# Matrices ahead, lag products, odd gates and the last norm of a two-layer mixer and expert trunk

## The reference, cut to what matters

```python
for i in range(2):
    hn = rms_norm(h, norm_mix[i])
    h = h + (chunked_rel_attention(hn, ...) if i == 0 else s5_mixer(hn, ...))
    hn = rms_norm(h, norm_ffn[i])
    h = h + hierarchical_moe(hn, ..., w_gate[i], w_up[i], w_down[i])
return rms_norm(h, norm_final)          # h * rsqrt(mean(h*h) + 1e-6) * g

# hierarchical_moe, after routing (best of 4 groups, best 2 of its 8 experts)
for e in range(32):
    hid = silu(t @ w_gate[e]) * (t @ w_up[e])      # 1024 x 256 each
    out = out + gates[:, e:e + 1] * (hid @ w_down[e])   # 256 x 1024

# s5_mixer: 64 groups of 16 channels, each with 64 complex states
abar = exp((lambda_re + 1j * lambda_im) * step)
bbar = (abar - 1) / lambda * b
x_t = abar * x_(t-1) + bbar @ u_t ; y = Re(c @ x) + d * u
```

## Time and profile before

| | us |
|---|---|
| median of 3 executions | 711.55 (710.52 to 712.64) |
| profiled execution | 711.8 |
| its span on the core | 710.1 |
| PE busy in the span | 629.6 (89%) |
| share of the chain that ended last: PE, DMA, SP | 72%, 19%, 3% |
| mean granted clock of PE, of full speed | 0.942 |

### The profile page before, as it was taken

How to read it: one execution, slowest core, us unless ns; L and a number is a source line. 1 busy time by engine, 2 the same in 40 slices (tenths; PEclk the granted TensorE clock), 3 DMA queues, 4 the chain that set the end, 5 groups by cost and what they waited for, 6 DMA issues and landing times.

```text
span 710.1 us, 13191 instructions
## 1 busy us (share of the span) xinstructions
PE 629.6 (89%) x5567; PEld 404.3 (57%) x5567; DVE 193.9 (27%) x499; ACT 136.7 (19%) x301; POOL 190.2 (27%) x226
## 2 busy tenths in 40 slices
PE   7999999999999988989598889999999798796583
PEld 5888888876556656456163654456564365353140
DVE  3234233254231023103022770235203023002003
ACT  3111313232021011011014511122220012010003
POOL 1001120250699997970961000030000000000001
PEclk9999999999998999899799999997999999898688
DMA  9997976665999999999999379964899999999992
GB/s 313 344 327 148 366 214 222 254 242 220 414 420 405 393 423 421 420 422 421 423 389 381 127 241 420 422 255 174 323 425 368 422 419 420 420 421 420 420 397 80
DMA packets 86707, 244.20 MB, mean 344 GB/s; under 512 B 28053, under 2 KB 56949, under 8 KB 62581
## 3 DMA queue, kind: packets, MB, share of 16 engines
q1 hardware_dynamic: 85188, 237.50, 86.7%
q0 software_dynamic: 1056, 5.24, 1.9%
q10 hardware_dynamic: 400, 0.57, 0.3%
HBM read 239.08 MB, written 4.22 MB: 343 GB/s over the span
## 4 chain that ended last, share of the span: by engine, by line
PE 72%; DMA 19%; SPq 3%; ACT 2%; DVE 1%; issue 1%; POOL 0%; DVEq 0%; POOLq 0%; ACTq 0%
DMA ring<-in_moe_w_down 11%; PE ps L2002 10%; DMA ring<-in_moe_w_up 9%; PE ps L1722 8%; PE ps L2289 8%; PE ps L2042 7%; PE ps L1856 7%; PE ps L2062 4%; PE ps L1725 4%; PE ps L1783 4%; PE ps L1702 3%; PE ps L1852 2%; SPq L478 2%; PE ps L1823 1%; PE ps L1918 1%
## 5 line engine op out<-in xcount | busy, mean ns | idle before, releaser
L2002 PE MATMUL ps<-ring,xg 128*32 128x256 f32 x1808 | 120.9, 402 | 26.3 <-DMA ring<-in_moe_w_up 14.5
L2002 PEld LDWEIGHTS ps<-ring,xg 128*32 128x32 f32 x1808 | 66.4, 116 | 74.3 <-issue 47.1
L2042 PE MATMUL ps<-ring,hidT 128*32 128x512 f32 x488 | 67.5, 671 | 15.8 <-DMA ring<-in_moe_w_down 10.6
L2062 PE MATMUL ps<-y_sb,pickT 128*128 128x512 f32 x128 | 59.5, 605 | 3.4 <-DVE y_sb L1475 1.7
L861 POOL TENSOR_TENSOR xh<-x,normw 128x1024 f32<-128x1024 f32 x1 | 2.4, 2352 | 214.2 <-DVE x L1437 214.2
L1722 PE MATMUL ps<-xnT,ring 128*128 128x256 f32 x256 | 57.7, 381 | 1.0 <-ACT xnT L904 1.0
L2289 PE MATMUL ps<-ring,yT 128*128 128x512 f32 x128 | 55.6, 594 | 0.9 <-ACT yT L1087 0.9
L1722 PEld LDWEIGHTS ps<-xnT,ring 128*128 128x128 f32 x256 | 47.8, 190 | 8.6 <-ACT xnT L904 1.2
L1442 DVE TENSOR_TENSOR hid<-sg,ps 128x256 f32<-128x256 f32 (+1 forms) x18 | 7.2, 399 | 156.2 <-ACT sg L1004 143.6
L2042 PEld LDWEIGHTS ps<-ring,hidT 128*32 128x32 f32 x488 | 17.4, 121 | 50.7 <-issue 43.3
L1856 PE MATMUL ps<-pick,xn 128*128 128x256 f32 x192 | 44.0, 382 | 0.0
(11 more groups left out here) (376 smaller groups left out, 878.1 us busy)
## 6 DMA issues: line engine op xcount, KB each, us to landing
ring<-in_moe_w_up SPq DMA_DIRECT2D x59, 1024.0 KB, 17.2
ring<-in_moe_w_gate SPq DMA_DIRECT2D x57, 1024.0 KB, 13.2
ring<-in_moe_w_down SPq DMA_DIRECT2D x53, 1024.0 KB, 16.2
ring<-in_attn_w_qkv SPq DMA_DIRECT2D x11, 1024.0 KB, 11.6
ring<-in_moe_w_down SPq DMA_DIRECT2D x16, 512.0 KB, 12.5
ring<-in_ssm_w_out SPq DMA_DIRECT2D x8, 1024.0 KB, 12.4
ring<-in_attn_w_o SPq DMA_DIRECT2D x4, 1024.0 KB, 10.9
chunk_inputs<-turned POOLq DMA_DIRECT2D x3, 1024.0 KB, 11.1
```

The costliest lines, as they stand in the source:

```text
L2002: ins = mm(ps[CAP * h:CAP * (h + 1), GUB, F * half:F * (half + 1)], p.xg[:, c, CAP * (ROUND * r + h):CAP * (ROUND * r + h + 1)], w, start= ...
L2042: ins = mm(ps[CAP * h:CAP * (h + 1), DNB + b, :], hidT[:, r, j, CAP * h:CAP * (h + 1)], w, start=(j == 0), stop=(j == FT - 1), tile_positi ...
L2062: ins = mm(ps[:, u, :], p.pickT[rows, r, tt * P:(tt + 1) * P], y_sb[rows, r, 512 * b:512 * (b + 1)], start=(r == 0), stop=(r == p.rounds - 1))
```

## The change

**Layer 0.** Three MiB more are on chip ahead of the first turns: a gate and an up of turn 0 (`fore_gate`, `fore_up`) and two half ups of turn 1 (`fore_up_next`). The ring slot they leave takes turn 1's matrices early.

**Layer 1.** Turn 0's second gate goes to `fore_gate`, and two half ups of turn 1 go to places that are free by then; one MiB net. From turn 3 on, odd turns' gates go outside the ring, into the places of turn 1's matrices, and gates are loaded two turns ahead (`turn + 2`).

**Lag products.** They are interleaved with the ups of the octets' first rounds: piece 0 in turn 2, piece 2 in turn 4, piece 3 in turn 6; piece 1 in the gather of the spill pass. Four of them stand ahead of each four wide products (eight ahead of each two in the spill pass). PE waits for the piece's table first. The table is turned right behind the ups. Turn 7 of layer 0 now starts with the sum, then gates, `keep_warm`, ups. POOL's work is put in another order.

**Final norm.** In layer 1's turn 7 PE first multiplies the identity with `x[:, tt, 512:]` into banks 1 and 3, and the last sums are added on top; ACT squares these columns out of PSUM, and DVE scales them out of PSUM. The norm's weights are multiplied by -0.5 by POOL ahead of time, which spares a step.

```diff
-WARM = {"start": 2, "choice": (5, 3), "ranks": 1, "regrouping": 1, "last lags": 4}
+WARM = {"start": 2, "choice": (5, 3), "ranks": 1, "regrouping": 1, "last up": 4}
...
+        fore_gate = at("fore_gate", [P, MAT], 6656)
+        fore_up = [(at("fore_up0", [P, MAT // 2], 4096), normw), (q4, normw)]
+        fore_up_next = (q4, at("fore_up_next", [P, MAT // 2], 10784))
...
+        def odd_gates(layer, turn):
+            return layer == 1 and turn >= 3 and turn % 2 == 1
+        odd_gate = [ahead_gu[1][:, 0:MAT], ahead_gu[1][:, MAT:], ahead_gu_next[:, 0:MAT], ahead_gu_next[:, MAT:]]
...
+                    elif not layer and s == RING - 1:
+                        gate_up(layer, first + ROUND + s, s, 0, slot_full[s])
+                    elif not (layer and s == 1):
...
+                def load_gate(at, e):
+                    turn, s = at
+                    if odd_gates(layer, turn):
+                        sp.dma_start(odd_gate[s], wg[:, bass.ds(E * layer + e, 1), :].rearrange("p o n -> p (o n)")).then_inc(odd_full, 16)
+                    else:
+                        gate_up(layer, e, s, 0, slot_full[s])
                 def places(turn, full):
                     kept = ahead_slots(full, layer, 1)
-                    if layer and full is slot_full and turn < 2:
-                        return [(2, s) for s in reversed(range(1, RING))] if turn == 0 else [(2, 0)]
+                    if layer and full is slot_full:
+                        if turn < 2:
+                            return [(2, 3), (2, 2)] if turn == 0 else [(2, 0)]
+                        return [(turn + 2, s) for s in range(RING)] if turn + 2 < 2 * NO else []
                     if turn == 0:
-                        return [(1, s) for s in range(kept, RING)] + [(2, s) for s in reversed(range(kept))]
+                        return [(1, s) for s in range(kept, RING) if not first_elsewhere(full, layer, s)]\
+                            + [(2, s) for s in reversed(range(kept))]
                     return [(turn + 1, s) for s in range(kept if turn == 1 else 0, RING)]
                 def load_behind(turn):
                     gates, ups, downs = (places(turn, full) for full in (slot_full, second_full, down_full))
-                    expert = {at: expert_at(*at) for at in dict.fromkeys(gates + ups)}
+                    behind_ups = [(3, s) for s in range(RING)] if layer and turn == 1 else []
+                    expert = {at: expert_at(*at) for at in dict.fromkeys(gates + ups + downs + behind_ups)}
                     held = turn == BLOCK_TURN
                     sp.wait_ge(S.first_done, k0 + turn + 1)
                     for at in gates[held:]:
-                        gate_up(layer, expert[at], at[1], 0, slot_full[at[1]])
+                        load_gate(at, expert[at])
                     sp.wait_ge(S.gu_done, k0 + turn + 1)
                     for at in ups[held:]:
-                        rows = slice(MAT // 2, MAT) if at == (1, 1 + layer) else slice(0, MAT)
+                        rows = slice(MAT // 2, MAT) if at == (1, 2 + layer) else slice(0, MAT)
                         gate_up(layer, expert[at], at[1], 1, second_full[at[1]], rows)
+                    for at in behind_ups:
+                        load_gate(at, expert[at])
...
+                if not layer:
+                    e = first + RING - 1
+                    sp.dma_start(fore_up[0][0][:], wu[:, e, 0:MAT // 2]).then_inc(fore_full, 16)
+                    sp.wait_ge(rows_ready, 2)
+                    sp.dma_start(fore_up[0][1][:], wu[:, e, MAT // 2:MAT]).then_inc(fore_full, 16)
+                    sp.wait_ge(ms_ready, 2)
+                    sp.dma_start(fore_up_next[0][:], wu[:, first + ROUND + 1, MAT // 2:MAT]).then_inc(ahead_full, 16)
                 if layer:
+                    sp.wait_ge(rows_ready, 5)
+                    sp.dma_start(fore_up[1][1][:], wu[:, E * layer + first + ROUND + 3, 0:MAT // 2]).then_inc(ahead_full, 16)
+                    sp.wait_ge(ms_ready, 4)
+                    sp.dma_start(fore_up[1][0][:], wu[:, E * layer + first + ROUND + 2, MAT // 2:MAT]).then_inc(ahead_full, 16)
...
+                if layer:
+                    gate_up(layer, expert_at(2, 1), 1, 0, slot_full[1])
...
+                pool.wait_ge(lags_evac, i + 1)
                 pool.wait_ge(tab_evac, 2 * (i + 1))
...
-            chunk_outputs((0, 1))
+            chunk_outputs((0,))
             store_inputs(0)
             chunk_inputs(1)
-            chunk_outputs((2,))
-            steps()
-            tables((1, 2, 4, 8))
+            chunk_outputs((1, 2))
             store_inputs(1)
             chunk_inputs(2)
-            tables((16,))
+            steps()
+            tables((1, 2))
             store_inputs(2)
             chunk_inputs(3)
+            tables((4, 8, 16))
...
+                    ins = nc.scalar.activation(xn[:, tt, 512:D], x[:, tt, 0:512], ACT.Square, accum_out=small[:, 7, tt:tt + 1])
+                ins.then_inc(rms_ready, 1)
+                act.wait_ge(main.comb_done, 4 * (2 * NO - 1) + 3)
+                nc.scalar.activation(xn[:, 0, 0:512], ps[:, 1, :], ACT.Square, accum_out=small[:, 0, 0:1])
+                act.wait_ge(main.comb_done, 4 * 2 * NO)
+                nc.scalar.activation(xn[:, 1, 0:512], ps[:, 3, :], ACT.Square, accum_out=small[:, 0, 1:2]).then_inc(rms_ready, 1)
...
+            def final_norm():
+                ss, ms, rt, r0, t1, rs, part = (small[:, j, :] for j in (0, 1, 2, 3, 5, 6, 7))
+                dve.wait_ge(rms_ready, 6)
+                lk(V.tensor_scalar(part, part, 1.0 / D, EPS, ALU.mult, ALU.add))
+                dve.wait_ge(rms_ready, 7)
+                V.scalar_tensor_tensor(out=ms, in0=ss, scalar=1.0 / D, in1=part, op0=ALU.mult, op1=ALU.add).then_inc(ms_ready, 1)
+                dve.wait_ge(rms_ready, 8)
+                lk(V.reciprocal(r0, rt))
+                for tt in range(TT):
+                    one = slice(tt, tt + 1)
+                    ins = V.scalar_tensor_tensor(out=t1[:, one], in0=ms[:, one], scalar=r0[:, one], in1=r0[:, one],
+                                                 op0=ALU.mult, op1=ALU.mult)
+                lk(ins)
+                V.scalar_tensor_tensor(out=rs, in0=t1, scalar=-3.0, in1=r0, op0=ALU.add, op1=ALU.mult).then_inc(rs_ready, 1)
+                dve.wait_ge(rs_ready, 3)
+                dve.wait_ge(rows_ready, 6)
+                for tt in range(TT):
+                    V.scalar_tensor_tensor(out=xn[:, tt, 512:D], in0=ps[:, 2 * tt + 1, :], scalar=rs[:, tt:tt + 1], in1=normw[:, 512:D],
                                            op0=ALU.mult, op1=ALU.mult).then_inc(xn_ready, 1)
...
+                        if beside:
+                            lag_products(beside, (2 * c, 2 * c + 1))
...
-            def lag_products(i, banks):
-
-                pe.wait_ge(tab_ready, i + 1)
-                for st in range(JP):
+            def lag_products(p, sts):
+                i = p.piece(0)
+                for st in sts:
                     for r in range(2):
-                        for par_g, bank in enumerate(banks):
+                        for par_g, at_lags in enumerate(lag_places(p)):
                             rows = slice(NS * par_g, NS * (par_g + 1))
-                            ins = mm(ps[:, bank, GC * st:GC * (st + 1)], wbt[rows, st, r].rearrange("p m c -> p (m c)"),
+                            ins = mm(at_lags[:, GC * st:GC * (st + 1)], wbt[rows, st, r].rearrange("p m c -> p (m c)"),
                                      wC[rows, 0, r, JP * i + st, :], start=(r == 0), stop=(r == 1), tile_position=(NS * par_g, 0))
-                return ins
+                    if st == JP - 1:
+                        ins.then_inc(lags_done, 1)
...
-                def gate_up(r, half, done):
+                def gate_up(r, half, done, beside=None):
                     for c in range(KT):
+                        if beside:
+                            lag_products(beside, (c,))
...
+                    if p.layer and p.closes(r):
+                        pe.wait_ge(before_p.S.x_added, 4 * before_p.n + 4)
+                        for tt in range(TT):
+                            mm(ps[:, 2 * tt + 1, :], ident, x[:, tt, 512:D], start=True, stop=False)
...
+                    sums_first = p.layer == 0 and p.closes(r)
+                    if sums_first:
                         pe.wait_ge(S.yh_done, p.k + r)
                         pe.wait_ge(S.yl_done, p.k + r)
-                        keep_warm(GUB, WARM["last lags"])
-                        lag_products(3, (DNB, DNB + 1)).then_inc(tab_turned, 1)
                         pe.wait_ge(before_p.S.x_added, 4 * before_p.n + 4)
-                        turn_chunk_inputs(0)
+                        combine(r - 1)
...
-                        if p.layer == 0 and p.closes(r):
-                            pe.wait_ge(tab_evac, 8)
-                        combine(r - 1)
+                        if sums_first:
```

(16 more changed lines are left out.)

204 lines of the change are left out of this document (110 added, 94 removed).

## The result

| | before | after |
|---|---|---|
| median | 711.12 us | 729.38 us |
| span of the profiled execution | 710.1 us | 726.9 us |

The medians are of four executions each. The changed kernel is slower: ratio 1.0253, 95% interval 1.0221 to 1.0285. The forecast was 706.5, with a range up to 713.5.

The account below looks back on a forecast made before the run. It took DMA's bytes, or time without bytes, to bound the kernel. Terms 0 + 2.2 + 1.8 + 1.1 = 5.1 us off the profiled 711.8 gave 706.7, as a median 706.5; range 699.5 to 713.5.

Parts of the forecast that it names:

- DMA's bytes bound both layers: Experts of both layers: only bytes, or time in which no byte moves, decide; a 1 MiB matrix costs 2.5 us.
- Layer 0's loads ahead: Layer 0, 3 MiB more on chip: counted as 0; 7.5 us the upper end if the saving survived.
- PE waits for the third piece's table in turn 4: Layer 0, turn 4: PE stalls some 5.5 us for POOL's table; DMA then idles some 2 us (0.6 to 4).
- The norm: Final norm at the kernel's end: ACT's square reads the bank directly, two small steps go; 1.1 us saved (0.8 to 1.4).
- a piece among the ups: Layer 0, one piece's lag products mixed with wide products: 3.0 us, between 0.7 and 4.3, or more if changes cost.
- a sign of being wrong: Layer 0: a piece of under 1 us or over 5 among the wide products would show the prediction wrong.
- PE's time is free: Where bytes decide, PE's time costs nothing until it delays the SP queue; PE busy 100 of 126 us in layer 1's stretch.
- the pieces ahead add about as much as their blocks took: Layer 0 before turn 4: mixed pieces cost about what their blocks did, so POOL's store starts from about 270.5.
- The slower rival: Layer 0: mixed lag products cost double, 7 us a piece, DMA idles 10 us behind turn 4's ups; about 714.5, chance 0.14.
- Turn 7 of layer 0: Lag block (3.75) and chunk turn (3.01) leave the path; second half starts near 380.0, a gain of 2.2 us.
- Layer 1: Layer 1's experts: second half of the downs starts 1.0 to 3.5 us earlier, 1.8 taken.
- the end of the bytes: Layer 1: bytes end 5 us earlier, from 2.5 us fewer bytes and 2.4 us of drained stretch filled.

Follow-up runs that it names:

- warm_short: The changed kernel with 6 wide identity products ahead of the lag products in turns 4 and 6 of layer 0; 719.94 us, ratio 1.0123.
- short_table_warm: Changed kernel, five of seven products of the third piece's table left out, 5 identity products in turn 6; 3497.7 us, only layer 0 read (last half 383.4).
- gates_last: Changed kernel with lag products, POOL's order and layer 0's turn 7 as before; layer 1's gates of turns 4 to 7 issued behind the preceding turn's downs; 704.95 us.
- lags_row: The changed kernel with a piece's 32 lag products in one row ahead of the ups, second piece still mixed; 723.42 us, ratio 1.0163.
- warm_before_lags: The changed kernel with 14 wide identity products ahead of the lag products in turns 4 and 6 of layer 0; 727.73 us, ratio 1.0224.
- gates_last_warm: gates_last with 4 identity products ahead of turn 6's ups and 2 ahead of its downs in layer 1; 706.73 us, ratio 0.9932.

## Why the prediction was wrong, point by point

**Right.** DMA's bytes bound both layers, and time without bytes is what counts. Layer 0's loads ahead are worth nothing (381.48 for 382.24 at the last half). PE waits for the third piece's table in turn 4: 5.5 us expected, 5.91 found, on the path that was written down (spill pass, evacuation, store, table). That the size came out so near is luck in part: both ends slipped alike, POOL's table from 285.6 to 292.2 and PE's readiness for it from 280.2 to 286.5. The norm: 1.1 expected, 1.35 found; from the last sum's end to the last multiplication 2.05 us, 2.3 expected.

```profile
716.27 1.95 PE L2165 MATMUL ps<-y_sb,pickT 128*128 128x512 f32 x4 [0.97 <-DVE y_sb L1543]
...
718.26 0.60 ACT L949 ACTIVATE xn<-ps 128x512 f32<-128x512 f32 x1 [0.17 <-PE ps L2165]
...
720.27 1.41 DVE L1252 SCALAR_TENSOR_TENSOR xn<-ps,small,normw 128x512 f32<-128x512 f32 x2
```

These rows answer: ACT's second square follows the sum's last bank directly, and DVE's add and square between them are gone.

**The term that failed: a piece among the ups, 3.0 us.** At full clock it is 5.4 (9.0 less 3.6), above the block's own 3.75, above the upper end of 4.3, and over the 5 that was written down as a sign of being wrong. By an estimate each of the 16 changes between narrow and wide costs about 0.1 us more, (9.0 - 3.6 - 3.75) / 16; the spill pass's mixture, with 8 changes, gives the same, (8.1 - 3.6 - 3.75) / 8, with 3.6 for its wide products alone. At the granted clock of 0.50 a piece is 12.2. The Trainium skill ("TensorE: Matmul & The Clock Gate", "Step-by-step: what each phase is for") has weight loads pulled ahead of running products where the row groups don't conflict or the load goes to the background buffer. The trace shows no time saved by that here, 9.0 us for the 7.35 of block and ups apart, and agrees with the same page's "The mechanism", where loads overlap only if row groups differ.

**The step that failed with it: PE's time is free, so its clock doesn't matter.** The prediction found the wait in turn 4 and charged it for itself alone. It saw in the earlier trace rows that a low clock follows a narrow block and in the earlier trace rows that products are slow behind a wait, and did not put the two together: behind a wait the mixture starts at the low clock, and it doesn't come back up, while the wide ups of before did within their own length (6.16 us behind 5.99 of waiting at 653.74; 3.66 at full clock). warm_short shows that this is about half of the loss, 8 to 11 us. So turn 4's ups were through at 308.2, not 292.2, DMA lost 14.3 us, not 2, and turn 6 repeated the low clock on PE's path.

Of the 16.0 us by which turn 4's ups were late, 9.2 are the mixture (15.8 for 6.6); 6.8 were there before it, which the prediction put at nothing ("the pieces ahead add about as much as their blocks took"). Turn 2's mixture kept its ups unread for longer, so SP issued turn 3's ups at 222.46 (216.92 before); PE waited 5.18 us for them, and they began at the low clock, 6.11 us for 3.66. And the spill pass's mixture took 8.1 us where its wide products alone take 3.6.

**The slower rival** named the place (turn 4's ups against the bytes in flight) and the sign, but its reason, a piece of 7 us at any clock, was wrong: it is 5.4 at the one level and 12.2 at the other. With the wait and at full clock (warm_short) layer 0's last half is still 11.4 us later than before, without the wait as well (short_table_warm) 1.2. Its 714.5 was too low, because it had nothing of the low clock and stopped at turn 4.

**Turn 7 of layer 0** did gain: from turn 6's downs to the last half 25.9 us for 35.4, more than the 6.8 of the two steps that left. It came after the loss, so nothing was left of it.

**Layer 1: 1.8 expected, -0.3 found** in this profile (-1.6 by 203.0, the middle of the five). Mechanism and order were right (turn 6's downs behind turn 7's gates, 23.1 to 25.6 us from there, 24.6 found). The term that was mis-sized is the end of the bytes, 5 us earlier, which put turn 6's downs 174.8 us behind the first gates; they came at 177.1. It was worked out as if DMA stayed full to the end, and the late ups and downs took that away. The order could be had without it, as gates_last shows.

## What to carry to other kernels

A wait of 5.9 us that the change added to PE cost here its own length and the low clock behind it; ask what runs next and whether that brings the clock up. Narrow products mixed with wide ones never brought it up here, so put them behind wide ones, not behind a wait. And where a prefetch queue is single, order it by who needs the data next: the same places with another order were worth 5 us.

## What had not been expected of the hardware

The mixture of narrow and wide products ran at 1.00 for 9.0 us in turn 2 and at 0.50 for 15.8 us in turns 4 and 6, with PE busy throughout both. Neither level changed within these, while with a row of narrow products alone the clock sank (0.68 over 10.6 us) and among the wide ups behind it it rose. The upper level is not safe in a mixture, though. That of the spill pass, 16 narrow records to 4 wide ones, held 1.00 for 8.1 us in the changed kernel, but in lags_row, warm_before_lags and warm_short, which have the same code there, it fell to the lower level in its second half (0.53 in the mean of 269.2 to 274.7 in warm_short), with no wait ahead, and in the last two turn 4's gates came 3.3 and 2.7 us later than in the changed kernel. Why it fell in some profiles only is open. From lags_row, the last of its four rows of lag products, where the first took 1.07:

```profile
270.78 1.89 PE L1996 MATMUL ps<-wC,wbt 64*128 64x16 f32 x16
```

Layer 1's routing, from its router to the first gates, takes from 13.3 to 17.2 us (15.6 in the changed kernel's profile), in kernels that do the same there: the window of 14 us from 476 shows clock 0.63 in the kernel before and in gates_last_warm, and 1.00 in gates_last. That alone is up to 3.9 us, beside a spread of single times of 706.6 to 713.5 for the kernel before, and it is why stretches between the same two instructions were compared here and not spans. The columns are time, PE busy, clock, DMA share, GB/s; in order the kernel before and gates_last (in gates_last_warm the clock is 0.63 again):

```profile
476.00:490.00 14.00, 13.58 (x53) 0.63 0.82 319
```

```profile
476.00:490.00 14.00, 12.60 (x86) 1.00 0.92 363
```
